# Two modulation rows leave TensorE's gate phases and are summed on VectorE

## The reference, cut to what matters

```
def modulation(cond, w, b):
    m = jax.nn.silu(cond) @ w + b          # w is 1024 x 6144
    return jnp.split(m[:, None, :], N_MOD, axis=-1)

sh1, sc1, g1, sh2, sc2, g2 = modulation(cond, p['mod_w'], p['mod_b'])
h = rms_norm(x, p['mix_pre_g']) * (1.0 + sc1) + sh1
y, state = rglru_mixer(h, ...)             # layer 0
x = x + g1 * rms_norm(y, p['mix_post_g'])
h = rms_norm(x, p['ffn_pre_g']) * (1.0 + sc2) + sh2
x = x + g2 * rms_norm(swiglu(h, ...), p['ffn_post_g'])
```

## Time and profile before

| | |
|---|---|
| median of three runs | 2269.2 us (2267.61 to 2272.26) |
| the profiled execution | 2266.86 us |
| its span in the profile | 2265.1 us |
| PE busy | 2231.6 us (99%) |
| DVE, ACT, POOL busy | 1374.7, 884.2, 713.9 us |
| granted clock of PE, mean | 0.997 |
| moved by DMA | 276.12 MB, mean 122 GB/s |

### The profile page before, as it was taken

The page is one execution under the profiler, slowest core; times in us unless marked ns, Lnnn a source line. Parts: engine busy times, 40 slices in busy tenths (PEclk is TensorE's granted clock), DMA queues, the critical chain, the costliest instruction groups (busy, mean ns, idle before and its releaser), DMA issues.

```text
span 2265.1 us, 31519 instructions
## 1 busy us (share of the span) xinstructions
PE 2231.6 (99%) x12816; PEld 2174.0 (96%) x12816; DVE 1374.7 (61%) x2288; ACT 884.2 (39%) x1226; POOL 713.9 (32%) x310
## 2 busy tenths in 40 slices
PE   8999999999999999999999999999999999999998
PEld 4988899999999999999999998999999999999998
DVE  6589855768757656533476687888365244443246
ACT  4587863344111111232353545654443323111134
POOL 3500021542121021332553545542353334121232
PEclk9999999999999999999999999999999999999999
DMA  9323233341433233433343454352343143321323
GB/s 306 120 76 106 96 129 138 127 152 63 134 109 125 94 98 112 132 129 103 112 140 122 150 171 136 130 198 80 124 155 131 56 135 126 112 75 56 102 94 121
DMA packets 211697, 276.12 MB, mean 122 GB/s; under 512 B 4776, under 2 KB 194784, under 8 KB 211040
## 3 DMA queue, kind: packets, MB, share of 16 engines
q1 hardware_dynamic: 183056, 224.36, 30.1%
q10 hardware_dynamic: 26768, 40.30, 5.1%
q0 software_dynamic: 1728, 9.44, 1.0%
HBM read 245.76 MB, written 28.32 MB: 121 GB/s over the span
## 4 chain that ended last, share of the span: by engine, by line
PE 85%; DVE 6%; issue 3%; ACT 2%; POOL 2%; DMA 1%; SPq 0%; ACTq 0%; POOLq 0%; DVEq 0%
PE bank L1042 82%; PE bank L1072 1%; DVE y L2142 1%; PE bank L1097 1%; POOL acc L2682 1%; POOL w_lo L2665 1%; ACT w_hi L1488 1%; DMA mod_stage<-in_l_mod_w 0%; DMA raw<-in_l_ffn_w_out 0%; DVE hid_lo L2465 0%; DVE pool_sum L2551 0%; DVE w_lo L2217 0%; PE bank L1117 0%; DVE y L2127 0%; DVE y L2485 0%
## 5 line engine op out<-in xcount | busy, mean ns | idle before, releaser
L1042 PE MATMUL bank<-mv_hi,w_hi 128*128 128x384 f32 (+2 forms) x2736 | 925.4, 338 | 7.6 <-ACT y L1808 4.1
L1042 PE MATMUL bank<-mv_lo,w_hi 128*128 128x384 f32 (+2 forms) x2736 | 918.4, 336 | 0.0
L1042 PE MATMUL bank<-mv_hi,w_lo 128*128 128x384 f32 (+2 forms) x2736 | 918.2, 336 | 0.0
L2665 POOL TENSOR_TENSOR w_lo<-raw,w_hi 128x2048 fp32r<-128x2048 f32 x106 | 491.4, 4641 | 1167.3 <-ACT w_hi L1488 1099.6
L1042 PEld LDWEIGHTS bank<-mv_hi,w_hi 128*128 128x128 f32 x2736 | 515.2, 188 | 14.0 <-issue 8.7
L1042 PEld LDWEIGHTS bank<-mv_lo,w_hi 128*128 128x128 f32 x2736 | 515.3, 188 | 0.8
L1042 PEld LDWEIGHTS bank<-mv_hi,w_lo 128*128 128x128 f32 x2736 | 515.1, 188 | 0.0
L1488 ACT ACTIVATE w_hi<-raw 128x2048 fp32r<-128x2048 f32 x159 | 299.6, 1908 | 393.1 <-DMA raw<-in_l_ffn_w_out 219.5
L1042 PE MATMUL bank<-hid_hi,w_hi 128*128 128x384 f32 (+2 forms) x1056 | 361.5, 342 | 6.4 <-DVE hid_lo L2465 3.1
L2485 DVE TENSOR_TENSOR y<-y,bank 128x384 f32<-128x384 f32 (+2 forms) x480 | 258.6, 553 | 160.3 <-PE bank L1042 160.3
L1042 PE MATMUL bank<-hid_hi,w_lo 128*128 128x384 f32 (+2 forms) x1056 | 355.7, 337 | 0.0
(11 more groups left out here) (163 smaller groups left out, 1831.5 us busy)
## 6 DMA issues: line engine op xcount, KB each, us to landing
raw<-in_l_ffn_w_in SPq DMA_DIRECT2D x92, 1024.0 KB, 5.1
raw<-in_l_ffn_w_out SPq DMA_DIRECT2D x46, 1024.0 KB, 4.9
raw<-in_l_mod_w SPq DMA_DIRECT2D x42, 1024.0 KB, 5.1
residual<-y ACTq DMA_DIRECT2D x10, 1536.0 KB, 6.9
x_old<-residual ACTq DMA_DIRECT2D x10, 1536.0 KB, 7.0
raw<-in_l_w_in SPq DMA_DIRECT2D x8, 1024.0 KB, 5.5
mod_stage<-in_l_mod_w SPq DMA_DIRECT2D x6, 1024.0 KB, 12.3
raw<-in_l_w_out SPq DMA_DIRECT2D x6, 1024.0 KB, 5.4
```

What stands on the lines that cost most here:

```text
L1042: last = pe.matmul(out, w, x, start=start and n == 0, stop=stop and n == len(steps) - 1)
L2665: pool.tensor_tensor(w_lo[:, slot(w), :], raw[:, q % 2, :], w_hi[:, slot(w), :].bitcast(F32), ALU.subtract).then_inc(w_lo_pool, 1)
```

## The change

Granules 14 and 15, the rows of phases (3, 0) and (3, 1), are no longer row and turn units on PE. DVE sums them like 16 to 19: 14 before the first product with `h_sum`, 15 and 16 behind that of branch 1, 17 behind that of branch 2. Their folds stand by hand before the first unit of branch 2 (14) and of branch 3 (15). SP's wait before a load changes with them: it waits for the sum and no longer for the turn. The banks of all later units move, since four units are gone. Granule 9 (branch 1) is split by ACT at the end of (3, 0) and by DVE in (3, 1), a phase later.

```diff
-FIRST_SUM = 16
+FIRST_SUM, BRANCH_SUMS = 14, 4
...
             m = FIRST_MODS + 2 * n + j
-            units += gate_units(n, j) + [("row", m, 0, 0)] + FILLS[n, j] + [("turn", m, 0, 0)]
+            if m < FIRST_SUM:
+                units += gate_units(n, j) + [("row", m, 0, 0)] + FILLS[n, j] + [("turn", m, 0, 0)]
+            else:
+                units += gate_units(n, j) + FILLS[n, j]
...
+                if (kind, n, j, g) in FOLD_BEFORE:
+                    pe.wait_ge(p_freed, UNITS_ON[MOD_BANK])
+                    mod_fold(FOLD_BEFORE[kind, n, j, g])
                 unit(u, as_split(0, g) if (kind, n, j) == ("rec", 0, 0) else {})
...
-                for m in range(FIRST_SUM, 20):
+                for m in range(FIRST_SUM + len(FOLD_BEFORE), 20):
                     yield
                     mod_fold(m)
...
-                evacuate_row(FIRST_MODS + pair)
+                if FIRST_MODS + pair < FIRST_SUM:
+                    evacuate_row(FIRST_MODS + pair)
...
-                    take_turn(FIRST_MODS + 2 * n + j)
+                    if FIRST_MODS + 2 * n + j < FIRST_SUM:
+                        take_turn(FIRST_MODS + 2 * n + j)
...
-                    if n >= 4:
+                    if m in (FIRST_SUM + 2, FIRST_SUM + 3) or m >= 20:
                         dve.wait_ge(mod_done, done_count(m - 2))
...
             dve.wait_ge(h_stored, 16 * KT)
+            mod_sum(FIRST_SUM)
             for n in range(3):
...
                 if n:
-                    mod_sum(FIRST_SUM + n - 1)
+                    mod_sum(FIRST_SUM + (1, 3)[n - 1])
+                if n == 1:
+                    mod_sum(FIRST_SUM + 2)
...
-                 ("gates", 1, 1): [7], ("gates", 2, 0): [8], ("gates", 2, 1): [9], ("gates", 3, 0): [],
+                 ("gates", 1, 1): [7], ("gates", 2, 0): [8], ("gates", 2, 1): [], ("gates", 3, 0): [9],
...
+FOLD_BEFORE = {("branch", 2, 0, 0): FIRST_SUM, ("branch", 3, 0, 0): FIRST_SUM + 1}
```

More of the change, by code:

```diff
@@ L543, in planned @@
     folded = [put(("PE", "mods", 0), 0.0, FOLD) for _ in range(2)]
-    for m in range(FIRST_SUM + 2, 20):
+    for m in range(FIRST_SUM + BRANCH_SUMS, 20):
         t = put(("DVE", "mods", 0), 0.0, MOD_SUM)
@@ L890, in mod_sums @@
         def mod_sums(m):
-            return (mod_sum_branch if m < FIRST_SUM + 2 else mod_sum_norms)[:, m % 2]
+            return (mod_sum_branch if m < FIRST_SUM + BRANCH_SUMS else mod_sum_norms)[:, m % 2]
         def norm_bank(g, n):
@@ L2748, in first_norms @@
                             pool.wait_ge(states_stored, 16)
-                            pool.wait_ge(mod_done, done_count(FIRST_SUM + 1))
+                            pool.wait_ge(mod_done, done_count(FIRST_SUM + BRANCH_SUMS - 1))
                         acc_tile(g, m)
```

## The result

The changed kernel takes 2270.91 us in the median of 21 runs (2268.09 to 2277.09); the kernel before took 2268.19 us beside it (21 runs, 2266.03 to 2272.26). The ratio is 1.0014, 95% interval 1.0008 to 1.0020: 3.2 us slower by the ratio, 2.7 by the medians. The forecast was 2268.9 us, a gain of 0.3 us, with a range of 2264 to 2274: the time lies in the range and 2.0 us above the forecast, but the kernel became slower where it was to become a little faster.

A forecast was written before the change was run, and what follows sets the result against it. PE, busy for 99% of the span, was taken as the bound. 4.15 - 1.7 - 1.6 - 0.4 - 0.2 = about 0.3 us gained: profiled 2266.86 becomes 2266.6, the median 2268.9 us; range 2264.0 to 2274.0.

The forecast's parts named there:

- PE's own work: Phases (3, 0) and (3, 1): two rows and turns removed, 7.6 us, two folds added, 1.6 us; worth 6.0 us.
- How much reaches branch 1: Start of branch 1: ACT's chain to the gelus lets it start only 4.15 us earlier; PE stands some 4.1 us.
- The clock: Behind the wait before branch 1: granted clock 0.83 over ten us, 1.7 us lost, with 0 as the other end.
- The folds: Before branches 2 and 3: two added folds of 0.79 us, hidden by nothing, 1.6 us lost.
- What the sums make late: Sums and loads from branch 2 on: in time for both folds, 0.4 us stall at the projection, 0 to 0.8 after.
- All of PE's work won: Rival at branch 1: ACT ready at 307.8, so all 6.0 us are gained, 2263.2 us; chance 0.12.
- The stall without echoes: Rival behind branch 1's wait: no clock drop and DVE in time, 2.5 us gained, 2266.7 us; chance 0.14.
- The load queue: Rival at branch 3 and the projection: SP's in-order loads make the sums a bound, 6.1 us lost, 2275 us; chance 0.12.

The follow-up runs named there:

- split early: The changed kernel with granule 9 split where the kernel before splits it (ACT at the end of (2, 1), DVE in (3, 0)): 2270.72 us, ratio 1.0012 to before.
- again: The changed kernel repeated word for word, nothing changed: 2270.02 us, ratio 1.0015 to the kernel before.
- the first experiment: Kernel before with only the row of (3, 0) taken out: granule 14 is a row in (3, 1), 15 is summed; 2269.84 us, ratio 1.0006.
- banks: The changed kernel with the banks of the units from branch 1 on rotated by two: 2271.29 us, ratio 1.0017 to the kernel before.
- filler: The changed kernel with 16 f32 matmuls of 128 columns on an idle bank in PE's wait before branch 1: 2273.31 us, ratio 1.0027 to before.

## Why the prediction was right or wrong, step by step

The stage went nearly as forecast. Mean of the three profiles of the changed kernel (first, split early, again) against 153.80:

- **PE's own work** (6.0 us net, 3.8 a row): branch 1 could start at the forecast wait. Right; the page has the 20 matmul instructions less.
- **How much reaches branch 1** (4.15 gained, 4.1 of waiting): it started 46.68 to 46.76 us after the first gate unit of (3, 0), before 50.72: 4.0 gained. The wait was 4.9 and not 4.1, because TensorE was through with its fills 0.6 us sooner than taken. That the row of (3, 1) was cover and not cost is shown by the two runs with one row each.
- **The clock** (1.7): branch 1 took 1.50, 1.54 and 2.72 us more than without a drop, mean 1.9. Right in kind, and in two of three in size; the profile compared first was the bad one.
- **The folds** (1.6): 0.79 us each in the chain, but the first matmuls of branch 1 and 2 are 25.87 us apart in the first experiment and 25.06 in before, those of branch 2 and 3 25.97 in after and 24.99 in before: 1.8 together.
- **What the sums make late** (0.4 at the projection, 0.2 at the fold of 18): nothing in these three profiles, since the second loads of the pairs landed in 10.6 to 10.7 and 7.7 to 7.9 us where 11.4 and 8.6 were taken. The order of the round was right. It is the next bound: as soon as TensorE comes 3 to 4 us earlier (banks, and in part the filler) it waits there.

4.0 - 1.9 - 1.8 = 0.3 us gained. The stage means 153.51 us, 0.3 less than before. That this is the forecast 0.3 to the tenth is in part luck: 0.6 us of late sums that did not come make up for 0.15 us less gained, 0.2 more clock and 0.2 more for the folds.

**The step that failed** is the last sentence of "What the sums make late", "Behind that, PE is the bound again and nothing of the plan changes". The plan did not change; the rest took 4.2 us more all the same (means 1849.4 and 1845.3). What the sum left out is that a shorter list of TensorE instructions moves the instruction packets against the loads behind them. About 1.4 of the 4.2 is the longer `hid_lo` wait (2.5 against 1.1) and 1.7 the drop behind it (the windows 1430 to 1440 of after: 10 x 0.17), 3.1 us together; 1 us is spread over other waits and drops, such as the one after the stall near 1604 us, which was the longer kind in two of three profiles against one of three. The first 267 us were also 1.2 us longer in the mean, within a scatter of 1.6 us among before's own. The profiles together give 5 us, the ratio over many runs 3.2: of the three profiled executions of the changed kernel two lay above their medians. In the mean over its 21 runs the changed kernel loses 13.3 us by clocks under 1 (one minus the granted clock, times the span), before 9.7 in the mean of the 120 runs beside the experiments; what is left of the time is 2255.9 us in both. So what the change gained in work and what it lost in waits cancel, and the loss has the size of the clock drops.

**The rivals.** All of PE's work won: no, ACT's serial chain stood where it was put. The stall without echoes: right on the sums (no stall in the stage), wrong on the clock. The load queue: not in the changed kernel, but in the two variants of it that took the stall at branch 1 or its drop away (banks, filler). The loss that came had no rival of its own: 0.12 was for slower by 4.5 us or more, and the mechanism there was another. That the time still lies in the range is luck too, since the range was drawn for other causes.

What stays open: how an instruction packet holds a load up, and why ffn_w_out lands 4.9 us after issue in one profile and 7.6 in another with the packet inside it in both; how the 3 us divide among the loads that meet a packet; and the first 267 us.

## What to carry to other kernels

Before taking work off the engine that is busy 99% of the time, ask what each piece covers: the same row of 3.8 us was worth 3.2 in one phase, as long as VectorE's sum was undisturbed, and less than nothing in the next, where the chain of another engine ended with it. When the work that is left is bound by several chains of nearly equal length, removing one stall only shows the next, and a new stall can cost a clock drop as well. And compare several profiles of each kernel from a fixed point before and after the change: a single one can be off by more than the change itself, and an instruction list that is shorter early on can change a stall a thousand microseconds later.

## What the runs showed of the hardware

- TensorE's own instruction loads are DMA traffic that a weight load can meet: 16 KB every 22 us, 101 times during the execution. The ffn_w_out load of 1 MB near 1409 us took 4.9 to 7.6 us with one inside (eleven profiles) and 4.8 to 4.9 without (seven).
- VectorE's sum (two inputs from SBUF) and GpSimd's split hold each other up, and which one suffers differs between executions of one kernel: 9.99 us for a sum of 5.63 (10.00 and 10.58 in two variants), or 10.88 for a split of 4.6 to 4.8. The Trainium skill, "SBUF — State Buffer", "Who interferes with whom", says that such a VectorE instruction contends with a GpSimd instruction that reads SBUF, as a lock for the whole instruction and not a division of speed; the one instruction of 4842 ns beside a split of 4.80 us agrees.
- The same stall of 4.9 us cost 1.5 us of clock in two executions and 2.7 in another; stalls of 1.2 to 1.55 us before branch 1 were followed by a full clock in the five profiles that had one, while the stall near 457 us of 1.88 us was followed by a drop in some executions and not in others.
